# A router's logits with the weights held in four column groups and the tokens moving

## The reference, cut to what matters

```python
x = layer_norm(DEEPNORM_ALPHA * x + mix, ln1_g[l], ln1_b[l])
logits = (x2d @ w_router).astype(f32) + router_bias      # [256, 1024] @ [1024, 16]
scores = softmax(logits)                                 # best of 4 groups, then its 2 best experts
...
f = sum over the 2 chosen experts of weight * (silu(x @ w_gate[e]) * (x @ w_up[e])) @ w_down[e]
x = layer_norm(DEEPNORM_ALPHA * x + f, ln2_g[l], ln2_b[l])
```

## Time and profile before

| | us |
|---|---|
| median of 3 runs | 2258.7 (2258.26 to 2258.95) |
| span of the profiled execution | 2261.8 |
| TensorE busy in it | 2213.9 (98%) |
| VectorE, ScalarE busy | 1144.6 (51%), 457.5 (20%) |

### The profile page before, as it was taken

The page is one execution under the profiler, slowest core; times in us unless marked ns, Lnnn a source line. Parts: engine busy times, 40 slices in busy tenths (PEclk is TensorE's granted clock), DMA queues, the critical chain, the costliest instruction groups (busy, mean ns, idle before and its releaser), DMA issues.

```text
span 2261.8 us, 24795 instructions
## 1 busy us (share of the span) xinstructions
PE 2213.9 (98%) x9825; PEld 1399.4 (62%) x9825; DVE 1144.6 (51%) x1926; ACT 457.5 (20%) x1046; POOL 3.1 (0%) x20
## 2 busy tenths in 40 slices
PE   8999999999999999999999999999999999999998
PEld 7755444544468765446444486788888888554453
DVE  3755775211137267763111247775556423587666
ACT  2001401211121014122111236420000102352110
POOL 0000000000000000000000000000000000000000
PEclk9999999999999999999999999999999999999999
DMA  8445934799983449435999902003222124403340
GB/s 345 149 178 218 385 141 175 285 399 426 428 358 134 164 155 422 167 149 216 392 425 428 420 33 113 1 1 112 75 75 89 52 103 180 155 10 149 140 177 19
DMA packets 38800, 454.71 MB, mean 201 GB/s; under 512 B 5288, under 2 KB 9242, under 8 KB 11034
## 3 DMA queue, kind: packets, MB, share of 16 engines
q1 hardware_dynamic: 35520, 449.85, 49.2%
q10 hardware_dynamic: 3162, 3.21, 0.4%
HBM read 452.00 MB, written 1.05 MB: 200 GB/s over the span
## 4 chain that ended last, share of the span: by engine, by line
PE 82%; DMA 8%; DVE 7%; DVEq 2%; issue 1%; ACT 1%; SPq 0%; ACTq 0%
PE banks L603 79%; DMA ring<-in_w_exp_up 7%; PE banks L1726 1%; PE banks L759 1%; DVE ring L3040 1%; DVE tiny L3250 1%; DVE tiny L2589 1%; DVE arena L2603 0%; DVE arena L3265 0%; DVE ring L2334 0%; DVE arena L2308 0%; DMA ring<-in_w_in 0%; DVE banks L2586 0%; DVEq L2309 0%; PE banks L1192 0%
## 5 line engine op out<-in xcount | busy, mean ns | idle before, releaser
L603 PE MATMUL banks<-ring,arena 128*64 128x512 f32 (+2 forms) x3302 | 960.7, 546 | 14.5 <-DMA ring<-in_w_exp_up 4.9
L603 PEld LDWEIGHTS banks<-ring,arena 128*128 128x128 f32 (+1 forms) x3302 | 449.5, 166 | 485.4 <-issue 450.7
L603 PE MATMUL banks<-arena 128*128 128x128 f32 (+7 forms) x1584 | 243.9, 344 | 3.7 <-issue 1.7
L603 PE MATMUL banks<-X,ring 128*128 128x256 f32 x1024 | 224.8, 382 | 0.8 <-DVE arena L2542 0.5
L603 PEld LDWEIGHTS banks<-X,ring 128*128 128x128 f32 x1024 | 195.8, 192 | 29.7 <-issue 2.3
L603 PEld LDWEIGHTS banks<-arena 128*128 128x128 f32 (+2 forms) x1584 | 155.3, 173 | 66.4 <-issue 34.9
L603 PE MATMUL banks<-arena,ring 128*128 128x256 f32 (+1 forms) x736 | 179.1, 399 | 0.1
L603 PEld LDWEIGHTS banks<-arena,ring 128*128 128x128 f32 x736 | 138.7, 190 | 36.8 <-issue 14.4
L2433 DVE TENSOR_TENSOR arena<-arena,banks 128x512 f32<-128x512 f32 x16 | 11.0, 687 | 281.9 <-ACT arena L1874 281.9
L603 PE MATMUL banks<-ring 128*128 128x256 f32 x616 | 137.0, 379 | 0.0
L603 PEld LDWEIGHTS banks<-ring 128*128 128x128 f32 x616 | 117.0, 190 | 16.3 <-issue 0.5
(11 more groups left out here) (369 smaller groups left out, 1923.6 us busy)
## 6 DMA issues: line engine op xcount, KB each, us to landing
ring<-in_w_in SPq DMA_DIRECT2D x38, 2048.0 KB, 11.8
ring<-in_w_exp_up SPq DMA_DIRECT2D x32, 2048.0 KB, 16.2
ring<-in_w_exp_down SPq DMA_DIRECT2D x32, 2048.0 KB, 12.3
ring<-in_w_exp_gate SPq DMA_DIRECT2D x30, 2048.0 KB, 13.5
ring<-in_w_ada SPq DMA_DIRECT2D x24, 2048.0 KB, 10.7
ring<-in_w_ffn SPq DMA_DIRECT2D x22, 2048.0 KB, 7.8
ring<-in_w_out SPq DMA_DIRECT2D x8, 2048.0 KB, 13.4
ring<-in_w_down SPq DMA_DIRECT2D x8, 1408.0 KB, 6.0
```

The source lines that it names most:

```text
L603: ins = nc.tensor.matmul(out, weights, moving, start=start, stop=stop)
```

## The change

Four things are changed together. The weights `wr` are padded by the host from 16 to 32 columns and laid out by partition, so that each partition's 256 values (1 KB) lie in one piece. The logits are computed with `wr`'s chunk stationary (32 columns) and the chunk's 256 tokens moving, chunk i of the order into column group i modulo 4, so that bank 4 holds four partial sums, experts on the partitions and tokens on the columns. ScalarE copies them to `part`. After `token_rows(0)`, `logits` adds the bias, sums the four groups and turns the result with one product a half: `part`'s 128 tokens stationary, the first 16 columns of `picks` moving, into bank 6, which VectorE now reads in place of bank 4.

```diff
-        wr = sb("wr", [P, DC, EXPERTS])
+        wr = sb("wr", [P, DC, 2 * EXPERTS])
...
-                def logits(tc):
-                    at_ = EXPERTS * tc
-                    mm(bank[4][:, at_:at_ + EXPERTS], ones[0:1, :], rbias[0:1, :], start=True, stop=False)
+                def logit_parts():
+
+                    C.next("norm", DC // 2)
+                    C.next("norm_v", DC // 2)
                     for i, k in enumerate(NORM_ORDER):
                         norm_chunk(k)
-                        ins = mm(bank[4][:, at_:at_ + EXPERTS], X[:, k, tc * P:tc * P + P], wr[:, k, :],
-                                 start=False, stop=(i == DC - 1))
-                    return ins
+                        g = 32 * (i % 4)
+                        ins = mm(bank[4][g:g + 32, 0:T], wr[:, k, :], X[:, k, 0:T], start=(i < 4), stop=(i >= 4),
+                                 more=(i < DC - 1))
+                    full(ins, 4, "act")
+                    return last[4]
+
+                def logits(parts_copied):
+
+                    free(6)
+                    for tc in range(TC):
+                        at_ = EXPERTS * tc
+                        mm(bank[6][:, at_:at_ + EXPERTS], ones[0:1, :], rbias[0:1, :], start=True, stop=False)
+                        if tc == 0:
+                            pe.wait_ge(*parts_copied)
+                        ins = mm(bank[6][:, at_:at_ + EXPERTS], part[:, tc * P:tc * P + P], picks[:, 0:EXPERTS],
+                                 start=False, stop=True)
+                    full(ins, 6, "dve")
...
                 turned_rows(xres, 1)
-                logits(0)
-                full(logits(1), 4, "dve")
+                parts_copied = logit_parts()
                 token_rows(0)
+                logits(parts_copied)
                 filler(0, 4, 6)
                 token_rows(1)
...
-            act.dma_start(wr[:], a["w_router"].rearrange("(k p) n -> p k n", p=P)).then_inc(s_params, 16)
+            act.dma_start(wr[:], a["w_router"]).then_inc(s_params, 16)
...
                     turned_rows(0, l, tc)
+                act.wait_ge(s_full["act"], C.next("full_act"))
+                done(nc.scalar.copy(part[:, 0:T], bank[4][:, 0:T]))
                 for i in range(2 * TC):
                     copy_chunk(xtok[:, i // 2, 512 * (i % 2):512 * (i % 2) + 512], 512)
...
-                v.tensor_reduce(t_(30), both(bank[4][:, 0:2 * EXPERTS]), AX_X, ALU.max)
-                done(v.tensor_copy(r_(0), bank[4][:, 0:2 * EXPERTS]))
+                v.tensor_reduce(t_(30), both(bank[6][:, 0:2 * EXPERTS]), AX_X, ALU.max)
+                done(v.tensor_copy(r_(0), bank[6][:, 0:2 * EXPERTS]))
...
+    router = np.asarray(inputs["w_router"]).reshape(DC, P, EXPERTS).transpose(1, 0, 2)
+    inputs["w_router"] = np.pad(router, ((0, 0), (0, 0), (0, EXPERTS)))
```

## The result

The changed kernel takes **2265.5 us** in the median of 6 runs (2263.4 to 2268.0) against 2258.8 for the kernel before on the same chip (6 runs, 2257.5 to 2259.3): a ratio of 1.003 with an interval of 1.0019 to 1.0042, so it is slower by 6.7 us. The forecast was 2255.0 with a range up to 2258.0 and a chance of 0.03 for slower. The profiled execution was the fastest of them, 2263.4 us; its span is 2261.6, so a time is 1.8 us more than the span that goes with it (the same in most runs here). By that measure the first profile of the kernel before, with its span of 2261.8, was an execution of some 2263.6 us, 4.9 above its median and not 3.1.

A forecast was written before the change was run, and what follows sets the result against it. TensorE was taken as the bound, busy 2213.9 of 2261.8 us. Two router gains of 2.7 us and one clock fall (-5.4 + 1.7 = -3.7) took 2258.7 to 2255.0 us, range 2252.6 to 2258.0.

The forecast's parts named there:

- Does a gain here reach the end?: Experts behind the router: loads and products both move by what the router gains, so the gain passes whole in both layers.
- the one that ended slower: Rival: half clock after the ranks lasts 6.8 us a layer in dense products, costing 6.8 against 5.4; 2260.1 us, chance 0.04.
- the gain of 2.7 us a layer: Router: ranks start at 401.19 in place of 403.89, the same in layer 1, 5.4 us in all.
- the distance to the median: Unprofiled median lies 3.1 us below the profiled span; kept, so the gain is taken off 2258.7 us.
- Part 6: Clock around the ranks: about even chance of falling in each layer, 1.7 us a fall; one fall of two expected, chance 0.42.
- Part 1: Router's group products: 16 records overlap four at a time, ending at 394.96, some 0.6 us after ScalarE's last chunk.
- Part 2: ScalarE's PSUM copy of the logits: 0.37 us, ending near 395.46, covered by 8 transposes, so the wait costs nothing.
- Part 3: Router's fold: 8 records in 0.88 us to 396.71; VectorE starts at 396.91, choice of experts ready at 401.19.
- Part 4: TensorE after the fold: filler and transposes to 399.30, then 1.9 us waiting for the choice; ranks start at 401.19.
- Part 5: Load of the router's weights at the start: 128 runs of 1 KB replace 1024 of 64 B; worth zero.

The follow-up runs named there:

- 192 signals: Changed kernel with 192 added TensorE semaphore increments, 48 ahead of each of layer 1's last four expert pairs: 2282.3 us.
- 48 signals: Changed kernel with 48 added TensorE semaphore increments, 12 ahead of each of layer 1's last four expert pairs: 2257.25 us.
- The second profile: Kernel before, unchanged, profiled once more: 2258.6 us, span 2257.7.
- the run with the weights in one piece: Kernel before with only the router's weights laid out by partition on the host, 16 columns as before: 2258.4 us.
- 198: Layer 1's branch place in the changed kernel with 24 added TensorE semaphore increments, 6 ahead of each of its last four expert pairs: 2265.4 us.
- 182: Layer 1's branch place in the kernel before without three of eight logits chunks' products in each half, waits kept: 2261.4 us.
- 110: Layer 1's branch place in the changed kernel with 192 added TensorE semaphore increments: 2282.3 us.
- 174: Layer 1's branch place in: changed kernel, 2265.5 us; changed kernel with filler ahead of the choice wait, 2260.3; kernel before without three logits chunks and their waits, 2261.6.
- 30: Layer 1's branch place in the changed kernel with 112 added TensorE semaphore increments, 28 ahead of each of its last four expert pairs: 2259.1 us.

## Why the prediction was wrong

**The step that failed** is the second section, "Does a gain here reach the end? ... I pass the gain on whole, in both layers." It looked at the load-bound part of the experts and was right about that: from the first load that waits for the router to the compare behind the experts it takes 225.3 to 226.7 us in both layers of the kernel before, of the changed one and of all the others but the one with 192 signals. What it didn't look at is what removing instructions does to the program behind them. The pause and its half clock cost 7.9 us in the trace; the run with 48 signals, which differs in those signals and so in the branch's place alone, is 8.2 us faster (2265.5 against 2257.25). No rival had it: the one that ended slower had its place in the router and put half clock behind the ranks.

**The second error is a size: the gain of 2.7 us a layer.** Without the pause the change is worth about 1.5 to 1.8 us, not 3.7. The forecast took both routers of the profiled execution as the rule, 6.8 us of half clock in each, and took the result off the median, 3.1 us below. The second profile and the run with the weights in one piece show where part of that distance was: one short stretch instead of a long one leaves 10.5 us to the ranks in place of 12.2. Most of the rest lay outside the routers: 1.5 us at the start and 0.9 in layer 1's experts. Against such a router the changed one saves 0.65 us (9.89 against 10.54), not 2.3. With one long and one short stretch the two layers give 0.65 + 2.6 = 3.3 us, and of that goes 1.7 for each time that the clock falls behind the ranks. So a part of the half clock was counted twice, in the terms and in the distance to the median. By the count under Part 6 (6 of 14 layers) the clock falls behind the ranks 0.86 times in an execution, which costs 1.5 us and leaves 1.8: an estimate from these rows, and what the runs without a pause show. The interval of each of these runs alone is still some 2 us wide to either side.

Part 1: the group products ended 0.67 us after ScalarE's last chunk (393.46 against 391.28 + 1.51 = 392.79), forecast 0.6. They overlapped: four weight loads of one pair of chunks every 0.35 us, where one by one four records would take 0.86. The Trainium skill's rule (TensorE: Matmul & The Clock Gate, Part 3, The mechanism), that a weight load overlaps only products of another row group, is not borne out by these rows.

Part 2: right. The copy ran from 393.50 to 393.87 under the transposes, and nothing waited for it.

Part 3: too cheap. Eight narrow records of bias and fold took 1.12 us (394.48 to 395.60), not 0.88 (the row it was read from has 0.97 for eight); the eight transposes ahead of them 1.02, not 0.87. VectorE began 0.4 us later than forecast, measured from the end of the second half's transposes (4.5 against 4.1 us).

Part 4: right but for that. VectorE's steps took 4.2 us, TensorE idled 1.58 us for them (1.9 forecast), and the ranks came 8.8 us after the transposes' end (8.4). The gain against a router with the long stretch was 2.3 and 2.6 us, forecast 2.7. (The two routers lie 635 us apart, 403.89 and 1039.10, not 632; nothing hangs on it.)

Part 5: right. The run that changed only the load's layout was the same as the kernel before.

Part 6: right as a chance. In the seven profiles of the changed router with its filler in place the clock fell behind the ranks in 6 of 14 layers, each time for 3.4 us (in neither layer of the changed kernel's own profile). With the filler moved into the idle time it fell in none of 4. The cost of the 1.6 us of idle, which the forecast named, was thus also the opportunity: filling it gave 4.3 us.

**What stays open** is the rule that decides when the load is asked for. Between places 198 and 200 it turns sharply, and a load follows 3.5 to 4.2 us behind the jump in all profiles but that at 182, in time or not. One reading, worked out after the runs, fits the turn. From the compare to the jump TensorE executes 56 entries in both layers of every profile, and 256 - 56 = 200. From place 200 on the jump itself stands in the stretch of 256 behind the compare's; below 200 it stands in the compare's own. The jump passes some 360 entries, so its target lies two stretches behind the jump's own at 110, 174, 182 and 198, where TensorE stood in the jump, and only one behind it at 30 and from 200 on, where it didn't. No run tests this by moving the jump's target, or the path that is jumped over, without the branch. It doesn't tell why the load began at the jump at 182, or why one execution of ten at 198 took as little time as without a pause: something that differs between executions has a say too.

## What to carry to other kernels

A change that only removes instructions can make a kernel slower at a branch far behind it: where the chain of waits shows "issue" for several microseconds at the end of a conditional part, look at the queue of instruction loads between the compare and the jump before blaming the change. Test it with a few dozen signals placed where the engine has slack, which move the code and little else (up to 28 in a row cost nothing here); four of them decided over some 8 us. Look at the times of all executions as well: the profiled one may be the one without the pause. And before taking a stage's time off a median, see whether the stage looks the same in a second profile of the same kernel.

## What the runs showed that was not expected

TensorE stood still for 5.4 to 5.9 us for its own instructions at a jump over some 360 entries, and half clock for 6.8 us came on top (10.2 in one run), some 8 us together. Where there was no pause, one load of 16 KB had begun about 1 us after the compare. Up to 28 signals in a row cost nothing where TensorE had slack; 48 in a row left it idle for 3.2 us. The length of a stretch of half clock in one and the same stage differs from execution to execution, 3.4 or 6.8 us, in steps that are worth 1.7 us.
